# Norms by halves of the tokens, FFN width in three chunks and a ring of eight split weights, in a two-layer encoder trunk

## Chip, cores and metric

The kernel runs on one core of a Trainium2 chip. The metric is the device time of one execution in microseconds (us), the median of several runs of the kernel.

## The reference

Two layers over 576 tokens: 512 of a prompt and 64 of a sample with cached states, with the same weights. All is float32. Each sub-layer has a norm ahead of it and one behind it:

```python
h = rmsnorm(x, norm_pre[l, 0])
x = x + 0.5 * rmsnorm(swiglu(h, ffn1_gu[l], ffn1_down[l]), norm_post[l, 0])
h = rmsnorm(x, norm_pre[l, 1])
...
mix = jnp.concatenate([sb_out, conv_out, o_hg], axis=-1) @ w_out[l]
x = x + rmsnorm(mix, norm_post[l, 1])
h = rmsnorm(x, norm_pre[l, 2])
x = x + rmsnorm(memory_attention(h, mem_k[l], mem_v[l], w_mq[l], w_mo[l]), norm_post[l, 2])
h = rmsnorm(x, norm_pre[l, 3])
x = x + 0.5 * rmsnorm(swiglu(h, ffn2_gu[l], ffn2_down[l]), norm_post[l, 3])
```

`rmsnorm(x, g)` is x · rsqrt(mean(x²) + eps) · g over the 1024 features, and `swiglu` is (silu(h W_gate) · (h W_up)) W_down with a width of 2816. The mixer between `h @ w_in` (26 × 128 columns) and `w_out` has a stick-breaking attention, a short convolution and a gated recurrence. The memory attention has keys and values of 256 memory tokens (`w_mk`, `w_mv`, from a normed memory) for the prompt and cached ones for the sample.

## The kernel before

All activations are feature-major: a tile [128, 8, 576] holds 8 blocks k of 128 features for 576 tokens. A float32 product is made of three fp32r products: weights and activations are split into a high and a low part, and hi·hi, lo·hi and hi·lo are added up in PSUM.

A **unit** is 128 output features of one projection. Its weights (128 × 1024 for 8 blocks k, 128 × 1408 for half of the FFN's width) are loaded into `raw` by SyncE's queue; ScalarE rounds them to `w_hi` (L855), VectorE subtracts to `w_lo` (L1183), and TensorE makes 3 products for each k and each half of the tokens (288 columns), 48 in all for 8 blocks k (`unit`, L372 to L390). The ring has two places; ScalarE's and VectorE's `step(u)` split unit u + 1 when unit u is done (L862, L1189). For the memory's keys, values and queries there are three places.

The order of the work is written out by hand, engine by engine; each queue goes through the phases F1, D1 (FFN up and down), IN, mixer, OUT, MK, MV and MQ in turns, cross-attention, MO, F2, D2, twice. The FFNs are loops (`Fori`).

At the end of a sub-layer every output tile is squared by ScalarE from PSUM (L906), GpSimd adds the squares up (L1597) and VectorE scales the tile by its gain into y (L1222). Behind the last unit, TensorE sums over the features by one-column products (`mean_square`, L411), ScalarE estimates the root by Ln and Exp (L900, L901), VectorE refines it (L1209 to L1214), TensorE spreads it over the partitions (`spread`, L420), and ScalarE copies it to `rinv` (L903). Then, for each k and all 576 tokens, y·rinv is made by VectorE for even k (L1227) and by GpSimd for odd k (L1605), VectorE updates x (L1231), ScalarE makes h_hi (L888) and the square for the next norm (L889), VectorE makes h_lo (L1196). The first unit of the next block waits for h_hi and h_lo per k:

```python
def h_gate(pn):
    def gate(ready, k):
        pe.wait_ge(ready, KD * pn + k + 1)
    return gate
```

The norm ahead of a sub-layer multiplies outputs, not h: its root is made beside the second unit (L401) and applied when a tile leaves PSUM. Around MK the updates stand between the units' splits on VectorE. The transposes of the sample's cached keys and of the new memory rows stand between the score products of the cross-attention (L782, L791). At the end, x is transposed (L832) and stored per block of 128 tokens.

## Time and profile before

| | |
|---|---|
| median of 3 runs | 3103.36 us (3102.82 to 3107.18) |
| span of the profiled execution | 3090.4 us |
| median less that span | 13.0 us |
| TensorE busy (20794 products) | 2920.0 us, 94% |
| VectorE, ScalarE, GpSimd busy | 1311.8, 943.6, 293.7 us |
| DMA | 232.84 MB, mean 75 GB/s |

The span is the time from the first to the last instruction of one profiled execution; no other time of that execution was recorded, so the median stands for it in the third line. Busy time is the time that an engine has an instruction under way; engines overlap, so the shares don't add up. The chain of work that ended last is followed back from the last instruction, and a wait is put down to the instruction that released it. The granted clock is the share of TensorE's full speed that the throttle allowed.

### The profile page before, as it was taken

Reading aid. Unit: us, or ns where it says so; the run is one execution under the profiler, and the core shown is the slowest. Engines: PE = TensorE matmul, PEld = TensorE weight load, DVE = VectorE, ACT = ScalarE, POOL = GpSimd, SP = SyncE. Lnnn points to the kernel's source line nnn. Section 1 sums busy time; section 2 is a strip of 40 time slices with the busy share of each in tenths; the row PEclk is TensorE's granted clock in tenths of the full one; section 3 lists DMA queues with packets and bytes.
Section 4 is the critical chain, followed back from the end, with each engine's and each line's share of the span. In section 5 each row is a group of like instructions: output and inputs, shape, how many; then the busy total and the mean of one; then the engine's idle time right before and its main releaser. Section 6 shows DMA issues by size and latency. Waiting matters only on the chain.

```text
span 3090.4 us, 49001 instructions
## 1 busy us (share of the span) xinstructions
PE 2920.0 (94%) x20794; PEld 2761.1 (89%) x20794; DVE 1311.8 (42%) x1583; ACT 943.6 (31%) x1218; POOL 293.7 (10%) x185
## 2 busy tenths in 40 slices
PE   8999998999989979999899999799999988999997
PEld 7999998985788879999899999799758978999996
DVE  5444226733363364442354432456343634544322
ACT  3222213225443232222232221232253432322211
POOL 1000012000120120000210001300102103100011
PEclk9999998997999989999899999799889998999998
DMA  3222221220242113232222232122203411222321
GB/s 111 81 81 87 85 75 56 62 88 21 75 123 89 45 51 88 82 89 85 65 68 81 81 88 85 46 76 62 88 1 103 124 61 55 68 81 81 88 85 50
DMA packets 420836, 232.84 MB, mean 75 GB/s; under 512 B 7076, under 2 KB 415688, under 8 KB 420712
## 3 DMA queue, kind: packets, MB, share of 16 engines
q1 hardware_dynamic: 414544, 210.33, 23.5%
q0 software_dynamic: 5936, 20.59, 1.9%
q8 instruction: 100, 1.64, 0.2%
q14 instruction: 24, 0.20, 0.0%
q10 hardware_dynamic: 232, 0.08, 0.0%
HBM read 219.44 MB, written 11.54 MB: 75 GB/s over the span
## 4 chain that ended last, share of the span: by engine, by line
PE 88%; DVE 7%; ACT 3%; issue 1%; DMA 1%; ACTq 0%; POOL 0%; DVEq 0%; POOLq 0%
PE PS L387 73%; DVE x L1231 2%; DVE y L1227 2%; PE PS L635 2%; PE PS L366 2%; DVE h_lo L1196 1%; PE PS L810 1%; PE PS L759 1%; PE PS L657 1%; PE PS L519 1%; PE PS L682 1%; DVE w_lo L1183 1%; PE PS L420 1%; PE PS L660 1%; PE PS L411 1%
## 5 line engine op out<-in xcount | busy, mean ns | idle before, releaser
L1183 DVE TENSOR_TENSOR w_lo<-raw,w_hi 128x1024 fp32r<-128x1024 f32 (+1 forms) x372 | 482.3, 1297 | 1271.4 <-ACT w_hi L855 1271.1
L387 PE MATMUL PS<-h_lo,w_hi 128*128 128x288 f32 x3904 | 848.1, 299 | 49.9 <-DVE h_lo L1196 49.6
L387 PE MATMUL PS<-h_hi,w_hi 128*128 128x288 f32 x3904 | 851.3, 300 | 26.0 <-ACT h_hi L888 21.5
L387 PE MATMUL PS<-h_hi,w_lo 128*128 128x288 f32 x3904 | 844.4, 298 | 0.0
L855 ACT ACTIVATE w_hi<-raw 128x1024 fp32r<-128x1024 f32 (+1 forms) x372 | 414.2, 1113 | 1246.8 <-PE PS L387 1246.4
L387 PEld LDWEIGHTS PS<-h_lo,w_hi 128*128 128x128 f32 x3904 | 635.9, 191 | 59.3 <-DVE h_lo L1196 59.3
L387 PEld LDWEIGHTS PS<-h_hi,w_hi 128*128 128x128 f32 x3904 | 638.2, 192 | 30.0 <-issue 22.3
L387 PEld LDWEIGHTS PS<-h_hi,w_lo 128*128 128x128 f32 x3904 | 638.8, 192 | 0.0
L1597 POOL TENSOR_TENSOR acc<-acc,sq 128x576 f32<-128x576 f32 x104 | 205.4, 1975 | 1862.6 <-ACT sq L906 1775.6
L387 PE MATMUL PS<-a_lo,w_hi 128*128 128x288 f32 x1408 | 300.4, 295 | 0.0
L387 PE MATMUL PS<-a_hi,w_lo 128*128 128x288 f32 x1408 | 300.3, 295 | 0.0
L387 PE MATMUL PS<-a_hi,w_hi 128*128 128x288 f32 x1408 | 300.2, 295 | 0.0
L387 PEld LDWEIGHTS PS<-a_hi,w_hi 128*128 128x128 f32 x1408 | 226.2, 188 | 0.0
L387 PEld LDWEIGHTS PS<-a_hi,w_lo 128*128 128x128 f32 x1408 | 226.2, 188 | 0.0
L387 PEld LDWEIGHTS PS<-a_lo,w_hi 128*128 128x128 f32 x1408 | 226.2, 188 | 0.0
L927 ACT ACTIVATE a_hi<-ut 128x576 f32 (+1 forms) x88 | 60.4, 687 | 258.8 <-DVE ut L1253 258.8
L920 ACT ACTIVATE sg<-gt 128x576 f32<-128x576 f32 x88 | 60.4, 687 | 176.1 <-DVE gt L1247 176.1
L1256 DVE TENSOR_TENSOR a_lo<-ut,a_hi 128x576 f32 (+1 forms) x88 | 66.7, 758 | 83.1 <-ACT a_hi L927 83.1
L366 PE MATMUL PS<-m_hi,w_hi 128*128 128x256 f32 x256 | 74.8, 292 | 12.7 <-DVE w_lo L1183 8.9
L1231 DVE SCALAR_TENSOR_TENSOR x<-y,x 128x576 f32<-128x576 f32 x64 | 85.7, 1352 | 1.1
L888 ACT ACTIVATE h_hi<-x,par 128x576 fp32r<-128x576 f32 x64 | 49.6, 775 | 96.1 <-DVE x L1231 87.9
L1222 DVE TENSOR_SCALAR y<-PS,par 128x576 f32<-128x576 f32 x64 | 52.0, 812 | 52.1 <-ACT sq L906 52.1
(286 smaller groups left out, 2843.7 us busy)
## 6 DMA issues: line engine op xcount, KB each, us to landing
raw<-in_ffn_gu_dram SPq DMA_DIRECT2D x176, 512.0 KB, 3.8
raw<-in_ffn_down_dram SPq DMA_DIRECT2D x64, 704.0 KB, 4.7
raw<-in_w_in_dram SPq DMA_DIRECT2D x52, 512.0 KB, 3.8
raw<-in_w_out_dram SPq DMA_DIRECT2D x16, 512.0 KB, 3.8
raw<-in_w_mk_dram SPq DMA_DIRECT2D x16, 512.0 KB, 3.8
raw<-in_w_mv_dram SPq DMA_DIRECT2D x16, 512.0 KB, 4.1
raw<-in_w_mq_dram SPq DMA_DIRECT2D x16, 512.0 KB, 3.9
raw<-in_w_mo_dram SPq DMA_DIRECT2D x16, 512.0 KB, 3.8
```

Source lines behind the costliest of these rows:

```text
L366: m = mm(out, lhs(a, k), rhs(b, k), start=(first and n == 0), stop=(last and n == 3 * kt - 1))
L387: m = mm(PL[slot][:, h, 0:HT], wt(ws)(a, k), (hi, lo)[b][:, k0 + k, h * HT:(h + 1) * HT], start=(first and n == 0), stop=(last and n == 3 ...
L635: mm(z[:, Z_OFF[j]:Z_OFF[j] + SEQ - j * P], proj[e:e + 64, K0 + h // 2, j * P:(j + 1) * P], proj[e:e + 64, Q0 + h // 2, j * P:SEQ], start= ...
L855: A(whi(s, slice(0, words)), rawu(s, slice(0, words)), ACT.Copy).then_inc(whi_r, 1)
L920: A(sg[:, :], gt[:, :], ACT.Silu).then_inc(sg_r, 1)
L927: A(a_hi[:, bass.ds(r, 1), :], ut[:, :].rearrange("p (o t) -> p o t", o=1), ACT.Copy).then_inc(ahi_r, 1)
L1183: TT(wlo(s, c), rawu(s, c), f32(whi(s, c)), ALU.subtract).then_inc(wlo_r, 1)
L1222: TS(halves(y[:, m, :]), PL[m % 2][:, :, 0:HT], gpost(l, pn % 4, m), None, ALU.mult).then_inc(tile_e, 1)
L1227: TT(y[:, k, :], y[:, k, :], rinv[:, :], ALU.mult).then_inc(y_r, 1)
L1231: STT(x[:, k, :], y[:, k, :], weight, x[:, k, :], ALU.mult, ALU.add).then_inc(x_r, 1)
L1256: TT(a_lo[:, bass.ds(r, 1), :], ut[:, :].rearrange(o1, o=1), f32(a_hi[:, bass.ds(r, 1), :]), ALU.subtract).then_inc(alo_r, 1)
L1597: nc.gpsimd.tensor_tensor(acc[:, :], acc[:, :], sq[:, c % 2, :], ALU.add).then_inc(acc_r, 1)
```

## The change

- **Halves.** Norm statistics, `rinv`, x, h_hi and h_lo are kept by halves of the tokens (288 each) with semaphores per half. The last projection of a sub-layer (the FFN's last down chunk, MO) runs all 8 units for the first half and then all 8 for the second (`ends_by_halves`); the next block begins with 8 (FFN) or 6 (IN) units for the first half and then for the second (`begins_by_halves`). A step of one half has 24 products and one PSUM bank. While TensorE makes the second half of the down product, the first half's norm and update go on; while it makes the first half of the next block, those of the second half. `PIECES` says beside which step which k is updated.
- **Norm.** Gains are applied with `rinv` in one instruction (`scale_y`), squares are taken of y in SBUF and added by VectorE (`add_square`), and the root is a bit estimate with three Newton steps on VectorE (`inverse_root`). Mean square and spread are products per half set between the products of a step. Every root is made by token now, that of the norm ahead of a sub-layer too.
- **Weights.** A unit has at most 8 blocks k; a ring of eight places holds split weights, with three `raw` buffers; tables built when the program is written say which unit is split after which step (5 and 3 steps ahead where units go by halves, else 3 and 2; a place must be free). In MK, MV and MQ the ring has three places.
- **FFN.** The width goes in chunks of 6, 8 and 8 blocks: gate and up, then a down product of the chunk, whose partial sums VectorE adds into y (`take_y`). All loops are written out.
- **Mixer to memory.** OUT keeps full width. The memory's transposes go beside OUT, the updates (`piece`) beside the 16 MK and MV units, then come 8 MQ units, with the transposes of cached keys and memory rows beside them.
- **GpSimd** only starts transfers. The output leaves per block of tokens, the first half's ahead.

The core of the diff:

```diff
-PHASES = [("F1", 2 * KF, KD), ("D1", 2 * KD, KU), ("IN", NIN, KD), ("OUT", KD, KD), ("MK", KD, KD),
-          ("MVQ", 2 * KD, KD), ("MO", KD, KD), ("F2", 2 * KF, KD), ("D2", 2 * KD, KU)]
+CHUNKS = (6, 8, 8)
...
+LAG_F, LAG_IN = 8, 6
+RING = 8
...
+        at_h = max(at_h, HELD[u], FIRST[u] - (5 if by_halves else 3))
+        at_l = max(at_l, at_h, FIRST[u] - (3 if by_halves else 2))
...
+PIECES = [(), (0,), (1, 2), (3,), (4, 5), (6,), (7,), ()]
...
+            def begins_by_halves(l, name, pn, lag):
+
+                post = 2 * pn - 1
+                for j in range(lag):
+                    beside = {}
+                    if j == 0 and pn:
+                        beside = {6: lambda: mean_square(post, 1)}
+                    elif j == 1:
+                        beside = {1: lambda: mean_square(2 * pn, 0), 6: lambda: spread(2 * pn, 0)}
+                        if pn:
+                            beside[3] = lambda: spread(post, 1)
+                    step(l, name, j, 0, h_hi, h_lo, gate=h_gate(pn, (0,)) if j == 0 else None, beside=beside)
+                for j in range(lag):
+                    beside = {}
+                    if j == 0:
+                        beside = {4: lambda: mean_square(2 * pn, 1)}
+                    elif j == 1:
+                        beside = {2: lambda: spread(2 * pn, 1)}
+                    step(l, name, j, 1, h_hi, h_lo, gate=h_gate(pn, (1,)) if j == 0 else None, beside=beside)
...
+            def inverse_root(r, a, t):
+
+                link(TS(r.bitcast(I32), a.bitcast(I32), 1, None, ALU.logical_shift_right))
+                link(TS(r.bitcast(I32), r.bitcast(I32), -1.0, ROOT_BITS, ALU.mult, ALU.add))
+                for n in range(3):
+                    link(TT(t, r, r, ALU.mult))
+                    link(STT(t, t, -0.5, a, ALU.mult, ALU.mult))
+                    ins = STT(r, t, 1.5, r, ALU.add, ALU.mult)
...
+            def ends_by_halves(l, name, pn, y_, weight, take):
...
+                for m in range(KD):
+                    turn(done(l, name, m, 1))
+                    take(m, 1)
+                    if m:
+                        add_square(n, m - 1, 1)
+                    for k in PIECES[m]:
+                        piece(pn + 1, k, 0, y_, weight)
+                    if m == 6:
+                        finish(pn + 1, 0)
+                add_square(n, KD - 1, 1)
+                newton(n, 1)
...
+                for n in range(2 * KD):
+                    turn(done(l, "MK" if n < KD else "MV", n % KD))
+                    if n == 1:
+                        piece(pn + 1, 0, 0, yh, 1.0)
+                        piece(pn + 1, 0, 1, yh, 1.0)
+                    elif n:
+                        piece(pn + 1, n // 2, n % 2, yh, 1.0)
```

Three places show how instructions moved. First TensorE, at the end of layer 0's first FFN. Before, the norm's products stood behind the last down unit and ahead of the first product of IN:

```order
L387 MATMUL PS<-a_lo,w_hi 128x288 x2
L411 MATMUL PS<-cst,acc 128x1 x5
L411 MATMUL PS<-cst,sq 128x1 x5
L420 MATMUL PS<-cst,small 128x128 x4
L420 MATMUL PS<-cst,small 128x64
L387 MATMUL PS<-h_hi,w_hi 128x288 x2
L387 MATMUL PS<-h_hi,w_lo 128x288 x2
L387 MATMUL PS<-h_lo,w_hi 128x288 x2
```

Now, in the first pass of IN (steps 0 and 1, first half; L449 is the mean square, L457 the spread):

```order
L432 MATMUL PS<-h_lo,w_hi_104 128x288
L449 MATMUL PS<-cst,acc 128x1 x3
L432 MATMUL PS<-h_hi,w_hi_104 128x288
...
L432 MATMUL PS<-h_lo,w_hi_105 128x288
L449 MATMUL PS<-cst,acc 128x1 x3
L432 MATMUL PS<-h_hi,w_hi_105 128x288
...
L457 MATMUL PS<-cst,small 128x128 x2
L457 MATMUL PS<-cst,small 128x32
L432 MATMUL PS<-h_hi,w_hi_105 128x288
```

The second half's norm behind the FFN is finished between products of IN's first half. Then VectorE behind the same down product; before, with the root's refinement (L1209 to L1214), one split and the updates of whole rows of tokens:

```order
L1222 TENSOR_SCALAR y<-PS,par 128x576 [waits square_ready,unit_products_done]
L1209 TENSOR_SCALAR small<-PS 128x5 [waits mean_square_ready]
L1211 TENSOR_TENSOR small<-small 128x5 [waits root_estimated]
L1212 TENSOR_TENSOR small<-small 128x5 [waits vector_step]
L1213 TENSOR_SCALAR small<-small 128x5 [waits vector_step]
L1214 TENSOR_TENSOR small<-small 128x5 [waits vector_step]
L1183 TENSOR_TENSOR w_lo<-raw,w_hi 128x1024 [waits w_hi_ready]
L1227 TENSOR_TENSOR y<-y,rinv 128x576 [waits rinv_ready]
L1231 SCALAR_TENSOR_TENSOR x<-y,x 128x576 [waits even_y_scaled]
L1231 SCALAR_TENSOR_TENSOR x<-y,x 128x576 [waits odd_y_scaled]
L1196 SCALAR_TENSOR_TENSOR h_lo<-x,par,h_hi 128x576 [waits h_hi_ready]
```

Now, one step of the second half of the down product (L1244 splits a weight, L1386 takes the step's tile into y, L1257 adds a square, L1286 scales y, L1297 updates x, L1280 makes h_lo; 0 and 1 at a semaphore's name are the halves):

```order
L1244 TENSOR_TENSOR w_lo_112<-raw_118,w_hi_104 128x1024 [waits w_hi_ready,step_products_done]
L1386 TENSOR_TENSOR y<-y,PS 128x288 [waits psum_tile_emptied]
L1257 TENSOR_TENSOR acc<-acc,sq 128x288 [waits squares_added1,square_ready1]
L1286 SCALAR_TENSOR_TENSOR y<-y,par,rinv 128x288
L1297 SCALAR_TENSOR_TENSOR x<-y,x 128x288 [waits y_scaled0]
L1280 SCALAR_TENSOR_TENSOR h_lo<-x,par,h_hi 128x288 [waits h_hi_ready0]
L1257 TENSOR_TENSOR acc<-acc,sq 128x288 [waits squares_added0,square_ready0]
```

The update of the first half stands between the takes of the second half. Last, VectorE in the memory's units; before:

```order
L1183 TENSOR_TENSOR w_lo<-raw,w_hi 128x1024 [waits w_hi_ready,unit_products_done]
L1227 TENSOR_TENSOR y<-y,rinv 128x576
L1231 SCALAR_TENSOR_TENSOR x<-y,x 128x576 [waits even_y_scaled]
L1196 SCALAR_TENSOR_TENSOR h_lo<-x,par,h_hi 128x576 [waits h_hi_ready]
L1183 TENSOR_TENSOR w_lo<-raw_93,w_hi 128x1024 [waits w_hi_ready,unit_products_done]
L1231 SCALAR_TENSOR_TENSOR x<-y,x 128x576 [waits odd_y_scaled]
```

and now:

```order
L1244 TENSOR_TENSOR w_lo_114<-raw_117,w_hi_106 128x1024 [waits w_hi_ready,step_products_done]
L1286 SCALAR_TENSOR_TENSOR yh<-yh,par,rinv 128x288
L1297 SCALAR_TENSOR_TENSOR x<-yh,x 128x288 [waits y_scaled0]
L1280 SCALAR_TENSOR_TENSOR h_lo<-x,par,h_hi 128x288 [waits h_hi_ready0]
L1257 TENSOR_TENSOR acc<-acc,sq 128x288 [waits squares_added0,square_ready0]
L1244 TENSOR_TENSOR w_lo_115<-raw_118,w_hi_107 128x1024 [waits w_hi_ready,step_products_done]
```

Each unit has the piece of one half now, over 16 units in place of 8, and the squares are added here and not on GpSimd.

## Rows read from the trace of the kernel before

**Rows 1.** The page: busy time of the engines, and the chain's shares by engine

```profile
PE 2920.0 (94%) x20794; PEld 2761.1 (89%) x20794; DVE 1311.8 (42%) x1583; ACT 943.6 (31%) x1218; POOL 293.7 (10%) x185
...
PE 88%; DVE 7%; ACT 3%; issue 1%; DMA 1%; ACTq 0%; POOL 0%; DVEq 0%; POOLq 0%
```

**Rows 2.** Waits of TensorE: us in total, times, longest

```profile
PE PS L387 <- DVE h_lo L1196: 49.6, 21, 2.7
PE PS L387 <- ACT h_hi L888: 21.5, 5, 4.3
```

**Rows 3.** Timeline of TensorE from F1 to IN: start, duration, instruction, wait

```profile
452.14 1.17 PE L411 MATMUL PS<-cst,acc 128*128 128x1 f32 x10
...
456.11 2.69 PE L420 MATMUL PS<-cst,small 128*128 128x128 f32 x10 [1.60 <-DVE small L1214]
463.10 0.82 PE L387 MATMUL PS<-h_hi,w_hi 128*128 128x288 f32 x2 [4.30 <-ACT h_hi L888]
...
476.32 0.85 PE L387 MATMUL PS<-h_lo,w_hi 128*128 128x288 f32 x2 [2.63 <-DVE h_lo L1196]
```

**Rows 4.** Windows: length, busy by engine, granted clock, DMA share, GB/s

```profile
463.10:488.70 25.60, 16.04 (x57) 14.06 (x58) 23.28 (x19) 10.95 (x16) 17.67 (x11) 0.51 0.01 3
488.70:495.10 6.40, 6.40 (x49) 6.34 (x48) 3.58 (x6) 1.80 (x3) 0.00 (x0) 1.00 0.28 82
...
1083.20:1118.50 35.30, 19.84 (x90) 17.31 (x88) 28.87 (x28) 14.52 (x22) 20.45 (x11) 0.56 0.05 15
```

**Rows 5.** Timeline of VectorE at the same boundary

```profile
455.28 0.17 DVE L1211 TENSOR_TENSOR small<-small 128x5 f32<-128x5 f32 x1 [0.57 <-ACT small L901]
455.48 0.17 DVE L1212 TENSOR_TENSOR small<-small 128x5 f32<-128x5 f32 x1
...
467.82 1.83 DVE L1231 SCALAR_TENSOR_TENSOR x<-y,x 128x576 f32<-128x576 f32 x1
469.58 0.81 DVE L1196 SCALAR_TENSOR_TENSOR h_lo<-x,par,h_hi 128x576 fp32r<-128x576 f32 x1
470.31 0.75 DVE L1231 SCALAR_TENSOR_TENSOR x<-y,x 128x576 f32<-128x576 f32 x1
...
487.56 1.22 DVE L1183 TENSOR_TENSOR w_lo<-raw,w_hi 128x1024 fp32r<-128x1024 f32 x1 [2.10 <-ACT w_hi L855]
```

**Rows 6.** Groups by line: busy us, mean ns of one, idle before and releaser

```profile
L1253 DVE TENSOR_TENSOR ut<-ut,sg 128x576 f32<-128x576 f32 x88 | 66.7, 758 | 10.1
L888 ACT ACTIVATE h_hi<-x,par 128x576 fp32r<-128x576 f32 x64 | 49.6, 775 | 96.1 <-DVE x L1231 87.9 <-DVE x L1280 7.4
L889 ACT ACTIVATE sq<-x 128x576 f32<-128x576 f32 x56 | 37.4, 669 | 0.0
L1482 DVE TENSOR_TENSOR at_c<-at_s,at_c 128x256 f32<-128x256 f32 x16 | 6.8, 424 | 0.6
```

**Rows 7.** Timeline of ScalarE at the same boundary

```profile
486.40 1.06 ACT L855 ACTIVATE w_hi<-raw 128x1024 fp32r<-128x1024 f32 x1 [2.18 <-PE PS L387]
```

**Rows 8.** Windows from OUT's end to MQ's end, columns as above

```profile
855.00:897.00 42.00, 33.30 (x240) 31.30 (x238) 34.19 (x40) 25.77 (x44) 16.20 (x12) 0.88 0.39 113
897.30:974.00 76.70, 75.75 (x580) 75.07 (x580) 30.93 (x31) 21.06 (x28) 1.15 (x1) 1.00 0.41 117
```

**Rows 9.** Timeline of TensorE in layer 0's cross-attention

```profile
974.80 7.17 PE L759 MATMUL PS<-mk_p,qx 128*128 128x256 f32 x32 [0.85 <-DVE qx L1544]
...
991.76 3.72 PE L759 MATMUL PS<-mk_p,qx 128*128 128x256 f32 x16 [0.69 <-ACT mv_p L1134]
```

**Rows 10.** Timeline of the end of the program

```profile
3056.26 1.17 PE L411 MATMUL PS<-cst,acc 128*128 128x1 f32 x10
...
3075.29 1.43 DVE L1231 SCALAR_TENSOR_TENSOR x<-y,x 128x576 f32<-128x576 f32 x2
```

**Rows 11.** The chain in order of time: two FFN's up products, start, length, count

```profile
37.11 415.20 PE PS L387 x3114
...
1118.87 404.93 PE PS L387 x3114
```

More of the change, by code:

```diff
@@ L583, in _ @@
                         beside[6] = head_squares
[L584 to L587 removed]
+                    step(l, "IN", m, None, h_hi, h_lo, beside=beside)
+                pe.wait_ge(tile_e, emptied(l, "IN", NIN - 2))
                 pe.wait_ge(hu_r, l + 1)
```

1170 lines of the change are left out of this document (597 added, 573 removed).

## The prediction

> **What bounds the kernel now.** The page's busy line and its chain of waits come first [rows 1]: TensorE is busy for 94% of the span, and 88% of the chain that ended last is TensorE. So only two things can move the time: time in which TensorE waits, and time in which it works below full clock. The table of waits [rows 2] says where it waits: 49.6 us for h_lo in 21 waits and 21.5 us for h_hi, both at the first unit after a sub-layer. The timeline of one such boundary [rows 3] shows the order: the down product ends at 452.14, the norm's small matmuls follow, the first product of the next block starts at 463.10, and then TensorE stops before pair after pair (2.63 us at 476.32). The table by windows [rows 4] has the second half of the loss: in 463.10 to 488.70 the granted clock is 0.51, the 1.2 GHz level, and right behind it, where products come without waits, it is 1.00, the 2.4 GHz level. From 452.1 to 488.7 are 36.6 us, in which 54 products of 0.133 us, 7.2 us, got done [rows 3, 4, 11]: a loss of 29.4 at such a boundary into the mixer (2 of them). Into an FFN it is 35.3 − 7.2 = 28.1 us (3 of them) [rows 4]. These five, 143 us, and the end of the program are what the change can gain. The same windows show VectorE busy for 23.28 of 25.60 us [rows 4], so VectorE sets that stretch.
>
> The unit of my sum is the profiled execution's span, 3090.4 us; the median of the three runs is 3103.36, 13.0 above it, and I carry these 13.0 over. Below 0.2%, 6 us, a measurement of this kernel can't be told from no change.
>
> **Prices of VectorE's halves.** 576 columns take 0.758 us and 256 take 0.424 [rows 6], so 1.04 ns a column and 0.16 us fixed: 288 columns take 0.46. With a gain from a pointer 0.81 for 576 becomes 0.51, and the x update 0.75 becomes 0.45 [rows 5]. Operations behind each other start 0.08 us before the end of the one ahead (469.58 + 0.81 against 470.31) [rows 5]. One piece, that is scale, x, h_lo and sum of squares for a half, is then 0.51 + 0.45 + 0.51 + 0.46 − 4 × 0.08 = 1.61 us. Before, the same x update took 1.83 us beside GpSimd's product and 0.75 without it [rows 5]; GpSimd computes nothing in the new kernel, so the low price holds throughout. The root is a chain of 12 tiny operations, each waiting for the one ahead, at the 0.20 us from 455.28 to 455.48 [rows 5]: 2.4 us, with the hand-overs around it 2.6, four times per boundary.
>
> The Trainium skill speaks against the halves (VectorE: DVE Perf Modes, section The TRN2 errata — SBUF-src ops pay a fixed extra latency per instruction): the latency is paid between instructions, so many small tiles pay it each, and it advises 512 elements or more. The 0.16 us fixed agree with that; the 0.08 by which a successor overlaps does not, and the sum goes by the rows. By the rule in full a piece is 1.93 and the sum 3049 in place of 3029: rival 2.
>
> **One boundary after the change.** Let 0 be the end of the down product's first half. The second half's 8 steps take 25.6 us (24 × 0.133 = 3.2 each), with norm matmuls in them about 27.1. The first half's root is ready at 4.9, spread and copied at 6.3, and the pieces begin behind the second take of y, at 8.0. From there VectorE has 6 takes (0.37), 6 sums (0.38), 8 pieces (12.5, since the first square needs no sum) and 4 splits (1.22 − 0.08 each) [rows 5]: 21.6 us, so it ends at 29.6. ScalarE makes h_hi and the squares in halves (0.78 and 0.67 us for the whole [rows 6]) between its splits of 1.06 [rows 7]; four such splits may each hold a piece up, by 0 to 1 us, I take 0.5: 31.6. TensorE wants the second half's mean square at k = 6 of the next block's first step, at 29.1 with its own detours: **a stall of 2.5 us**. Behind it, root (2.6), a split and another root stand in VectorE's line; TensorE reaches the first spread 2.0 and the second 1.2 us later, so 1.2 and 2.4 more. The second half's pieces, 12.5 plus 6 takes and a split, 16 us, run beside the rest of the first pass (14.8 us): about 1.0 at the mean square and 0.6 at the last spread. Stalls: 7.7. TensorE's four mean squares and spreads are 12 products of one column and 12 of 128: at 0.12 and, at the low level, 0.27 each [rows 3] 4.7 us, and about 3 at the high one; I take 3.4. For clock dips near the stalls I add 2.0. **Loss 13 us**, against 29.4 and 28.1. Gain 2 × 16.4 + 3 × 15.1 = 78. Bounds: stalls gone but the 3.4 and 1 left, 4.4; stalls and the low level, next part.
>
> **Memory keys and values.** Now the mixer's output norm runs in the 16 MK and MV units, one piece each. The order below the diff shows that unit n + 3's w_lo stands ahead of unit n's piece, and both its splits wait for unit n. Per unit: w_hi 1.06, w_lo 1.15, scale 0.43, x 0.37, ScalarE's h_hi and square 0.77, and some hand-overs: 3.9 us, where TensorE's 24 products of 256 columns, by their columns, need 2.84. So 16 × 3.9 + 10 for the two roots ahead = 73, and MQ (8 × 6.4, one wait of some 5 us) ends at 129.5, plus 2 for the memory's transposes beside OUT, against the 119.0 from 855 to 974 before [rows 8]. The cached keys' transposes move beside MQ: before, they stood between two score products, 9.8 us from 981.97 to 991.76 [rows 9]. Two MO splits queue ahead of the last query tile: 3.3. Net 12.5 − 9.8 + 3.3 = +6 a layer, **+12** (bounds −6 to +14 each: no lock-step at all, or TensorE at the low level for two units).
>
> **Start and end.** At the start a split and a root stand ahead of step 1's spread (1.2 + 2.6 + 0.7 copy): **+4.5**, 0 to 6. At the end, x's last tile was ready at 3076.7, 20.5 us behind the last product at 3056.26 [rows 10]; now 5.5 for the norm and 8 × 0.80 for scale and x make 11.9. What follows was 13.7 for five blocks of tokens; with three left 9.6. **−12.6** (−6 to −16).
>
> **Edits at nothing.** 32 more splits and the partial sums of y (16 per FFN at 0.76) lie beside steps of 4.8 and 6.4 us; if their cover went, 0.76 each, 49 us. Between chunks TensorE reaches the last k of a down step at 4.0 to 5.6 us, a_lo is there at about 4.3. Products and their weight loads are as many as before (a load stands with every matmul already). Loops unrolled: products inside the loops already come each 0.133 us [rows 11], so nothing. The other pace, 0.130 [rows 11], appears in one FFN of four; all four so would be −31, none +10.
>
> **Sum**: −78 + 12 + 4.5 − 12.6 = −74; 3103.4 − 74 = **3029 us**, own range 2998 to 3055.
>
> **Rivals.**
> 1. *Cover complete.* VectorE keeps up, MK and MV don't lock. For: 29.6 stands close to 29.1. Against: roots in one line with splits. Loss 4.4 per boundary: −(2 × 25.0 + 3 × 23.7) = −121, memory part −6.4 × 2 = −13, rest −8: 2961.
> 2. *Every half pays in full.* No overlap: 0.32 a piece, 2.6 us a pass, 8 passes with stalls: +20, 3049. For: the 0.16 fixed. Against: the 0.08. This is the page's rule.
> 3. *Some steps at the low level.* A step at 1.2 GHz costs 3.2 us more. With three such per boundary in place of the dips: 5 × 9.6 − 10 = +38: 3067.
> 4. *Slower: the low level from the first wait to the last.* Before, the clock stayed at 0.51 from the first wait to the last [rows 4]. After, waits stand from the next block's step 0 to the second pass's step 0: 6 steps into the mixer, 8 into an FFN, 2 × 6 + 3 × 8 = 36 steps, 115 us. Without dips the change gains 74 + 10 = 84, so it loses from 27 steps on; this gives 3103 − 84 + 115 = 3134. Against: between these waits lie 4 to 6 steps without any, and in 488.70 to 495.10 the level was 1.00 at once.
> 5. *The halves don't overlap at all*, since a wait holds a whole pass: the root's chain is merely moved, and the memory part cancels the end: 3100.
>
> **Chances.** Forecast 0.45, rival 1 0.23, 2 0.10, 3 0.09, 4 0.10, 5 0.03. Faster: 0.45 + 0.23 + 0.10 + 0.08 = 0.86; same 0.03; slower 0.11 (rival 4, 0.01 of 3). The range 2960 to 3085 takes in rivals 1 to 3 and leaves out 4, 5 and a tail below.
>
> **What would show it.** The waits for h_lo and h_hi at products nearly vanish; in their place stand waits of mean square and spread for acc and small, under 10 us per boundary. GpSimd has no arithmetic. In the windows of the new boundaries the clock is above 0.85. w_lo in MK and MV comes each 3.9 us. The last output leaves 22 us after the last product. I am wrong if a boundary loses over 20 us, if TensorE waits at down steps for y's takes or for splits, or if the clock stays near 0.5 in a by-halves pass.

## The result, and the profile after

The kernel takes **3051.09 us** (median of four runs, 3047.48 to 3056.27) against 3103.09 of the kernel before on the same chip: a ratio of **0.985, interval 0.9825 to 0.9875**. It is faster by 52 us, where 74 were forecast, and 3051 lies inside the forecast's own range.

The page, the line of the engines and the chain's shares [rows 1]:

```profile
PE 2922.1 (96%) x20906; PEld 2768.8 (91%) x20906; DVE 1442.7 (47%) x2585; ACT 971.1 (32%) x1456; POOL 32.0 (1%) x50
...
PE 87%; DVE 5%; ACT 3%; issue 3%; DMA 1%; ACTq 0%; DVEq 0%; POOL 0%; POOLq 0%
```

TensorE is busy for as long as before in a span of 3051.4 us, 39 shorter than that of before. GpSimd has only its transfers left. TensorE's waits (us in total, times, longest) [rows 2]:

```profile
PE PS L449 <- DVE acc L1257: 29.8, 14, 3.8
PE PS L412 <- ACT mk_p L1164: 11.7, 12, 1.5
PE PS L412 <- ACT mvT L1164: 10.5, 12, 0.9
...
PE PS L432 <- ACT a_hi L1003: 2.9, 4, 0.7
```

The 71 us of waits for h_hi and h_lo are gone, as the prediction's last part asked for; the mean square (L449) waits for its sum of squares instead. The windows of TensorE's waits, the products behind them and the stretch after that, from F1 to IN (length, busy by engine, granted clock, DMA share, GB/s) [rows 4]:

```profile
466.20:470.00 3.80, 0.16 (x2) 0.00 (x0) 3.21 (x6) 2.00 (x4) 0.71 (x1) 1.00 0.37 105
470.00:479.60 9.60, 9.58 (x49) 9.13 (x49) 7.09 (x30) 0.41 (x1) 0.00 (x0) 0.64 0.37 111
479.60:494.80 15.20, 15.20 (x117) 15.20 (x116) 13.87 (x33) 7.15 (x17) 0.00 (x0) 1.00 0.13 37
```

TensorE stands for 3.8 us, then works 9.6 us at a mean granted clock of 0.64, so that 0.36 / 0.5 of them, 6.9 us, were at 1.2 GHz; and then 2.4 GHz holds, where before 25.6 us were at 0.51. At the boundary from layer 0's second FFN to layer 1's first, the stretch behind a wait of 3.8 us:

```profile
1532.80:1543.80 11.00, 10.96 (x48) 10.55 (x48) 7.13 (x30) 2.26 (x3) 0.00 (x0) 0.53 0.31 91
```

By the same working 10.3 us are at 1.2 GHz here. Counted alike in both kernels (from 192 products ahead of the down's end to the 288th product of IN, or the 384th of an FFN, less 0.1333 us a product), a boundary into IN lost 29.6 us and now 13.7, one into an FFN 27.5 to 28.4 and now 14.9 to 15.9.

**Two paces.** One thing had to be taken out before stages could be compared. The chain's longest rows, the run of an FFN's gate and up products with the down products of its first two chunks (the rows of before [rows 11] hold down products too), read in the kernel after and in one of the experiments (newton2):

```profile
67.97 341.80 PE PS L432 x2562
```

```profile
1548.52 333.81 PE PS L432 x2562
...
2602.97 341.80 PE PS L432 x2562
```

The same 2562 products take 0.1334 or 0.1303 us each, at a granted clock of 1.00 both, and one program shows both in one execution. A whole FFN at the faster pace is 8 to 10 us shorter. The profiled execution of before had one such FFN of four (404.93 against 415.20 [rows 11]), that of after none; newton2 and late_pieces below have three. So stages are compared at the slower pace: 0.16 us are added for every 48 FFN products made at the faster one. The sums are then 3100.4 before and 3053.2 after, **47.2** apart; the rest of the 52 is put down to pace. (After has no fast FFN, yet its sum is 1.8 above its span: some of the half steps, at 0.1316 us a product in every kernel by halves, are counted as fast.) In this measure (stage ends at its last product; us):

| stage | before | after | mk_pieces_first | three_edits | three_edits + idle products |
|---|---|---|---|---|---|
| F1 and D1, layer 0, with the start | 452.1 | 464.3 | 463.6 | 465.1 | 463.5 |
| IN, layers 0 / 1 | 235.4 / 235.4 | 217.3 / 217.4 | 217.9 / 218.7 | 217.2 / 214.1 | 215.4 / 214.2 |
| mixer and OUT | 167.4 / 167.5 | 165.4 / 161.8 | 161.8 / 163.3 | 165.8 / 163.6 | 163.5 / 162.2 |
| MK, MV, MQ | 118.8 / 118.8 | 135.3 / 135.3 | 114.3 / 113.1 | 113.1 / 115.9 | 114.3 / 114.3 |
| cross-attention, MO | 109.3 / 109.2 | 106.2 / 106.2 | 106.3 / 107.7 | 107.7 / 109.8 | 106.5 / 106.6 |
| F2 and D2, layer 0 | 450.5 | 439.0 | 439.1 | 438.0 | 434.7 |
| F1 and D1, layer 1 | 450.8 | 440.0 | 439.9 | 438.1 | 434.6 |
| F2 and D2, layer 1 | 450.8 | 439.0 | 439.4 | 437.9 | 434.7 |
| behind the last product | 34.2 | 26.3 | 26.0 | 25.7 | 26.2 |
| sum | 3100.4 | 3053.2 | 3011.0 | 3011.8 | 2990.6 |

The last column is three_edits_filler. The mixer's stage scatters between executions of kernels that don't differ there, and with its clock: 153.9 us in late_pieces (layer 1), where 10.2 us of it are at 1.2 GHz, 161.8 in the kernel after (27.3) and 168.8 in masks_after_x (44.4). Two sums less than 15 us apart are therefore read at their boundaries, whose losses add up to 142.9 us before and 73.3 after. The memory's part, 33 us slower in the two layers, is the one place where the change costs a lot.

### The profile page after: what moved, and what is told of

Its sections match the earlier page's. It is cut to its first block, busy times and chain, and to the rows that moved or that the text cites. A ratio compares the mean times of both kernels' runs of the same rounds, so it can differ in the third digit from the quotient of the medians.

```text
span 3051.4 us, 48442 instructions
## 1 busy us (share of the span) xinstructions
PE 2922.1 (96%) x20906; PEld 2768.8 (91%) x20906; DVE 1442.7 (47%) x2585; ACT 971.1 (32%) x1456; POOL 32.0 (1%) x50
## 3 DMA queue, kind: packets, MB, share of 16 engines
q1 hardware_dynamic: 415056, 210.33, 23.9%
## 4 chain that ended last, share of the span: by engine, by line
PE 87%; DVE 5%; ACT 3%; issue 3%; DMA 1%; ACTq 0%; DVEq 0%; POOL 0%; POOLq 0%
PE PS L432 72%; ACT w_hi L912 2%; PE PS L681 1%; PE PS L836 1%; PE PS L868 1%; DVE w_lo L1244 1%; PE PS L703 1%; PE PS L457 1%; PE PS L566 1%; PE PS L728 1%; PE PS L449 1%; DVE x L1297 1%; PE PS L706 1%; DVE acc L1257 1%; DVE yh L1286 1%
## 5 line engine op out<-in xcount | busy, mean ns | idle before, releaser
L1244 DVE TENSOR_TENSOR w_lo<-raw,w_hi 128x1024 fp32r<-128x1024 f32 (+1 forms) x404 | 485.4, 1203 | 1162.3 <-PE PS L432 845.3
L432 PE MATMUL PS<-h_hi,w_hi 128*128 128x288 f32 x3904 | 911.4, 300 | 4.6 <-DVE x L1428 3.0
L432 PE MATMUL PS<-h_lo,w_hi 128*128 128x288 f32 x3904 | 899.8, 297 | 0.0
L432 PE MATMUL PS<-h_hi,w_lo 128*128 128x288 f32 x3904 | 899.8, 297 | 0.0
L1003 ACT ACTIVATE a_hi<-ut 128x576 fp32r<-128x576 f32 (+1 forms) x104 | 63.5, 610 | 151.8 <-DVE ut L1376 151.8
L1000 ACT ACTIVATE sg<-gt 128x576 f32<-128x576 f32 (+1 forms) x104 | 63.5, 611 | 137.5 <-DVE gt L1370 137.4
L1257 DVE TENSOR_TENSOR acc<-acc,sq 128x288 f32<-128x288 f32 x224 | 99.6, 450 | 2.3 <-ACT sq L941 2.0
L935 ACT ACTIVATE h_hi<-x,par 128x288 fp32r<-128x288 f32 x128 | 68.3, 534 | 100.2 <-DVE x L1297 88.2
L412 PE MATMUL PS<-m_hi,w_hi 128*128 128x256 f32 x256 | 75.7, 296 | 22.2 <-ACT mk_p L1164 11.7
L1363 DVE TENSOR_TENSOR a_lo<-ut,a_hi 128x576 fp32r<-128x576 f32 (+1 forms) x104 | 68.7, 661 | 39.7 <-PE PS L432 30.7
L1386 DVE TENSOR_TENSOR y<-y,PS 128x288 f32<-128x288 f32 (+1 forms) x96 | 52.8, 550 | 57.5 <-PE PS L432 57.5
L432 PE MATMUL PS<-xo_hi,w_hi 128*128 128x288 f32 x256 | 76.0, 297 | 3.6 <-DVE xo_lo L1705 3.6
```

What stands on the lines that cost most here:

```text
L412: m = mm(out, wt[a][:, k * P:(k + 1) * P], (hi, lo)[b][:, k0 + k, :], start=(n == 0), stop=(n == 3 * KT[u] - 1))
L432: m = mm(BK[bank][:, 0:HT], wt[a][:, k * P:(k + 1) * P], (hi, lo)[b][:, k, c * HT:(c + 1) * HT], start=(n == 0), stop=(n == 3 * kt - 1))
L935: A(h_hi[:, k, cols(h)], x[:, k, cols(h)], ACT.Copy, scale=gpre(pn // 4, pn % 4, k)).then_inc(hi_r[h], 1)
L1000: A(sg[:, cols(h)], gt[:, cols(h)], ACT.Silu).then_inc(sg_r, 1)
L1003: A(a_hi[:, u // 2, cols(h)], ut[:, cols(h)], ACT.Copy).then_inc(ahi_r, 1)
L1244: TT(w_lo[SLOT[u]][:, c], raw[u % 3][:, c], f32(w_hi[SLOT[u]][:, c]), ALU.subtract).then_inc(wlo_r, 1)
```

## The experiments

All are edits of the changed kernel; ratios stand to the kernel before.

### mk_pieces_first: the memory's circle broken on VectorE

```diff
                 for n in range(2 * KD):
-                    turn(done(l, "MK" if n < KD else "MV", n % KD))
                     if n == 1:
                         piece(pn + 1, 0, 0, yh, 1.0)
...
+                    turn(done(l, "MK" if n < KD else "MV", n % KD))
```

> In the memory's 16 units VectorE updates x (scale, x, h_lo, sum) ahead of the unit's split and no longer behind it. Theory, lock-step: the 3.98 us from one w_lo to the next (865.82, 869.80, 873.78) are one circle, w_hi on ScalarE, w_lo, scale and x on VectorE, h_hi and square on ScalarE; with the update ahead, w_hi and the update go side by side, VectorE needs 1.60 + 1.15 = 2.75 and TensorE's 2.84 decides: 14 units x 1.1 = 15 us a layer, 31 us in all, about 3021. Rival, evacuation: TensorE's waits are for ScalarE's copies of mk_p and mvT (11.7 and 10.5 us); the copies stay behind w_hi, so the waits stay and nothing changes (within 5 us). Rival, the wait moves: MQ's start waits for the roots anyway and gives half back, 15 us.

Measured: 3012.26 us (3009.19 to 3021.05), **0.9743 [0.9707, 0.9778]**; 3011.0 at the slower pace, 42 less than the changed kernel, where 31 were expected. MK, MV and MQ take 21 and 22 us a layer less. VectorE in the units of MK, in the changed kernel (start, duration, instruction, wait):

```profile
869.80 1.23 DVE L1244 TENSOR_TENSOR w_lo<-raw,w_hi 128x1024 fp32r<-128x1024 f32 x1 [1.53 <-ACT w_hi L912]
870.94 0.51 DVE L1286 SCALAR_TENSOR_TENSOR yh<-yh,par,rinv 128x288 f32<-128x288 f32 x1
871.37 0.45 DVE L1297 SCALAR_TENSOR_TENSOR x<-yh,x 128x288 f32<-128x288 f32 x1
...
873.78 1.23 DVE L1244 TENSOR_TENSOR w_lo<-raw,w_hi 128x1024 fp32r<-128x1024 f32 x1 [1.52 <-ACT w_hi L912]
```

ScalarE in the same units:

```profile
871.86 0.54 ACT L935 ACTIVATE h_hi<-x,par 128x288 fp32r<-128x288 f32 x1 [1.89 <-DVE x L1297]
872.30 0.43 ACT L936 ACTIVATE sq<-x 128x288 f32<-128x288 f32 x1
872.63 1.04 ACT L912 ACTIVATE w_hi<-raw 128x1024 fp32r<-128x1024 f32 x1
873.58 0.36 ACT L1164 ACTIVATE mk_p<-PS 128x256 f32<-128x256 f32 x1
```

The split waits for w_hi, w_hi stands behind the square of x, x stands behind the last split: 3.98 us around, with both engines waiting for each other 1.5 to 1.9 us each time. The copy that empties TensorE's bank goes around with it, and that is the wait for mk_p and mvT. VectorE of this experiment has no such wait, and its splits come 2.87 us apart:

```profile
867.93 1.23 DVE L1244 TENSOR_TENSOR w_lo<-raw,w_hi 128x1024 fp32r<-128x1024 f32 x1
...
870.81 1.23 DVE L1244 TENSOR_TENSOR w_lo<-raw,w_hi 128x1024 fp32r<-128x1024 f32 x1
```

The window of 13 units, in which TensorE has no gap (columns as above):

```profile
857.90:895.30 37.40, 37.40 (x314) 37.40 (x313) 35.96 (x64) 27.38 (x53) 0.00 (x0) 1.00 0.64 183
```

So 2.87 is what TensorE needs. Of the 21 us, 15 are the units (67.2 to 52.5 us from MK's start to MQ's) and 6 are MQ behind them (67.9 to 61.7). Those 6 are a stall and the clock again. In MQ of the changed kernel:

```profile
920.34 0.83 PE L449 MATMUL PS<-cst,acc 128*128 128x1 f32 x6 [3.13 <-DVE acc L1257]
```

```profile
920.30:929.00 8.70, 8.66 (x44) 8.66 (x45) 4.70 (x27) 1.06 (x1) 0.00 (x0) 0.61 0.15 43
```

The last updates come late there, TensorE waits 3.13 us for their sum of squares, and 6.8 us behind the wait are at 1.2 GHz, which costs 3.4. In this experiment there is no wait at that place, and the clock stays at 1.00.

### mk_copy_first: the same stage, the other engine

```diff
-                    turn(done(l, "MK" if n < KD else "MV", n % KD))
+                    act.wait_ge(unit_d, done(l, "MK" if n < KD else "MV", n % KD))
                     A((mk_p if n < KD else mvT)[:, n % KD, :], PL[n % 2][:, 0, 0:NMEM], ACT.Copy).then_inc(mkv_e, 1)
+                    turn(done(l, "MK" if n < KD else "MV", n % KD))
```

> In the same units ScalarE copies mk_p and mvT out of PSUM ahead of the next w_hi and not behind it. Rival, evacuation: TensorE's 22.2 us of waits for these copies go, 3029. Theory, lock-step: the circle of 3.98 us doesn't hold the copy's place (0.36 us lie beside VectorE's work), w_hi even comes 0.36 us later in it; the waits only change their name, to w_lo: 0 to +10 us.

Measured: 3053.64 us (3040.72 to 3059.47), 0.9866 [0.9827, 0.9905]; MK, MV and MQ 139.7, 4.4 longer a layer. Expected was that the waits for the copies would go or turn into waits for w_lo; they stay, 26.8 us against 22.2. The copy stands behind the square of x now and so still goes around with the circle, which grows by it from 3.98 to 4.24 us (w_lo at 868.90 and 873.14). That the wait for mk_p is a sign of the circle and no cause of its own is shown by mk_pieces_first: there the copies stand behind w_hi as in the changed kernel, and TensorE waits for none.

### late_pieces: the overlap taken away

```diff
-PIECES = [(), (0,), (1, 2), (3,), (4, 5), (6,), (7,), ()]
+PIECES = [(), (), (), (), (), (), (), (0, 1, 2, 3, 4, 5, 6, 7)]
...
-                    if m == 6:
+                    if m == 7:
                         finish(pn + 1, 0)
```

> All eight updates of the first half stand behind the last take of the second pass (one change of the table, with the last h_lo behind them): the cover of the second pass is taken away, the rest of the change stays. Theory, cover is what the change gains: 12.5 us of VectorE's work per boundary come onto TensorE's path, at half clock in part: 5 x 12 to 15 us, 60 to 75 us more, about 3118. Rival, the gain is from GpSimd's arithmetic gone and shorter instructions: the first products of the next block need the updates only k by k, 1.6 us each against 0.4 us of products: 5 x 5, 25 us more, about 3078.

Measured, a single run: 3079.45 us with three FFNs at the faster pace, 3102.6 at the slower one. That is 49 above the changed kernel and 2 above the one before; expected were 60 to 75 more, or 25. A boundary loses 24.2 to 24.8, 10 more (49 in all), the end takes 7 longer, and the mixer of layer 1 happened to be 8 shorter. TensorE at the first boundary:

```profile
466.24 0.58 PE L432 MATMUL PS<-h_hi,w_hi 128*128 128x288 f32 x1 [3.94 <-ACT h_hi L935]
...
469.63 0.61 PE L432 MATMUL PS<-h_lo,w_hi 128*128 128x288 f32 x1 [0.51 <-DVE h_lo L1280]
...
477.12 1.44 PE L449 MATMUL PS<-cst,acc 128*128 128x1 f32 x6 [2.09 <-DVE acc L1257]
```

The waits for h_hi and for pair after pair of h_lo are back [rows 3], those for h_lo shorter (0.5 us for 2.7 at most). So 49 of the 70 us that the boundaries gained are the updates beside the down product's second half. The other 20 stay without that overlap: a boundary still loses less than the 27.5 to 29.6 of before, with 20.5 to 23.9 us at 1.2 GHz where before there were 30.7 to 34.1. Which part of the change brings these 20 (halves, the new root, no arithmetic on GpSimd), no run separates. The whole time is back at that of before because the memory's part and the start cost about as much as these 20 give.

### squares_first, hi4, newton2: what makes the stall

The chain that ended last through the stall (start, length, what):

```profile
464.21 3.80 DMA raw<-in_w_in_dram
...
469.05 0.43 ACT sq L941
469.51 0.47 DVE acc L1257
470.02 0.83 PE PS L449 x6
470.85 1.85 PE PS L432 x9
472.70 1.07 PE PS L449 x6
473.77 1.65 PE PS L432 x6
475.42 1.42 PE PS L457 x6
476.84 2.01 PE PS L432 x9
478.84 0.78 PE PS L457 x6
479.62 15.24 PE PS L432 x114
```

A weight's load ends ahead of ScalarE's last square, and this gave two theories: the load holds ScalarE's queue up, or VectorE has too much ahead of the last sum. squares_first puts the squares ahead of the splits:

```diff
-                    turn(s + 1)
                     post_square(pn, y_, s, m, 1)
+                    turn(s + 1)
...
-                    turn(done(l, name, m, 1))
+                    v.wait_ge(unit_d, done(l, name, m, 1))
                     take(m, 1)
                     if m:
                         add_square(n, m - 1, 1)
+                    if m == KD - 1:
+                        add_square(n, KD - 1, 1)
+                    turn(done(l, name, m, 1))
```

> In the second pass of a down product VectorE takes y and adds squares ahead of its split, and ScalarE squares y ahead of its split; nothing else moves. Theory, a late weight: the 3.8 us stall at the mean square of the second half comes from a raw buffer freed late, whose load lands at 468.01 and holds ScalarE's queue, with the last square behind it; with the square ahead, the stall falls to about 1 us: 5 boundaries x 2.5 to 3, 12 to 15 us less, about 3037. Rival, VectorE's work (the step of the prediction): VectorE has 21.6 us of work from 8.0 on and more by hand-overs, so the end of the sums only changes its place with a split: 0 to 5 us less.

Measured: 3048.81 us (3045.83 to 3056.44), 0.986 [0.9824, 0.9896]; 3051.1 at the slower pace; waits for acc 27.3 us, the longest 4.3. The order alone does next to nothing: at four boundaries the stall is 2.8 to 2.9 us in place of 3.5 to 3.8, and the five lose 71.3 us in all against 73.3. At the first boundary, with the 4.3, a late load stood in ScalarE's queue one step earlier, so this left the load open.

hi4 lets ScalarE split four steps ahead where units go by halves, so that each load has a step more:

```diff
-        at_h = max(at_h, HELD[u], FIRST[u] - (5 if by_halves else 3))
+        at_h = max(at_h, HELD[u], FIRST[u] - (4 if by_halves else 3))
```

> Where units go by halves, w_hi is made 4 steps ahead and not 5; w_lo stays 3 ahead. So the raw buffer is asked for one step later, and its load (freed by the w_lo of three units before, 3.8 us to landing) is there when ScalarE comes to it. Theory, a late weight: ScalarE's waits for loads in the second passes (464.66 and 468.09 at the first boundary) go, the last square comes in time, and the stall at the second half's mean square (3.8 us) falls to about 1: 12 us less in all at the same pace of the products. Rival, VectorE's work: 21.6 us from 8.0 on are there whatever ScalarE does; the stall keeps 2.5 us or more: 0 to 6 us less.

Measured: 3035.70 us (3026.68 to 3048.87), 0.9799 [0.976, 0.9838]; 3048.4 at the slower pace, with 72.0 us at the boundaries. ScalarE's 66.5 us of waits for the weights of down, MO and IN are gone, and the stall is not: 26.8 us in 14 waits. VectorE ahead of one, and TensorE's wait:

```profile
1084.83 1.21 DVE L1244 TENSOR_TENSOR w_lo<-raw,w_hi 128x1024 fp32r<-128x1024 f32 x1
...
1088.66 1.22 DVE L1244 TENSOR_TENSOR w_lo<-raw,w_hi 128x1024 fp32r<-128x1024 f32 x1
1089.80 0.45 DVE L1708 COPY yh<-PS 128x288 f32<-128x288 f32 x1
1090.16 1.05 DVE L1257 TENSOR_TENSOR acc<-acc,sq 128x288 f32<-128x288 f32 x2
```

```profile
1091.27 1.44 PE L449 MATMUL PS<-cst,acc 128*128 128x1 f32 x6 [3.04 <-DVE acc L1257]
```

VectorE has no gap up to the last sum, and TensorE waits 3.04 us for it, here and at the other four boundaries: the bound that the prediction named, without any load. The load that ended in the chain only came on top.

newton2 leaves out one of the root's three Newton steps (its output is coarser), 3 of 12 chained operations:

```diff
-                for n in range(3):
+                for n in range(2):
...
-                    if n < 2:
+                    if n < 1:
                         link(ins)
```

> Two Newton steps per root and not three (so a coarser root): each chain of tiny operations loses 3 x 0.20 = 0.6 us. Theory of the prediction (the roots stand in line on TensorE's path, two of them behind the stall of each boundary): 2 x 0.6 per boundary, 2 x 0.6 at each layer's memory part, 0.6 at start and end: 6 + 2.4 + 1.2 = about 10 us less at the same pace. Rival, the roots are covered by products: 0 to 2 us less.

Measured: 3031.92 us (3021.40 to 3037.63), 0.9788 [0.9756, 0.9821], with three FFNs of the profile at the faster pace; 3049.7 at the slower one, 3.5 less than the changed kernel. Boundaries into an FFN lose 13.8 to 15.1 against 14.9 to 15.9, those into IN 13.4 and 14.2 against 13.7: 1.8 less in all five, where 6 were expected if the roots stood on the path. The 3.5 of the sum is less than the mixer's scatter, so no more than those 1.8 can be read.

### squares_gpsimd: the arithmetic given back to GpSimd

```diff
-                add_square(2 * pn, k, h)
...
+                        nc.gpsimd.tensor_tensor(acc[:, cols(h)], acc[:, cols(h)], sq[:, k % 2, cols(h)], ALU.add).then_inc(acc_r[h], 1)
```

> The squares of the norm ahead of a sub-layer are added by GpSimd again (112 of 224 sums), VectorE makes the others. VectorE is rid of 14 x 0.37 = 5.2 us per boundary. Theory of the prediction (low prices hold since GpSimd computes nothing): beside a GpSimd sum, VectorE's half operations grow as 0.75 grew to 1.83, that is 0.45 to about 1.1; a sum takes GpSimd about 1.0, so some 14 us of VectorE's time per boundary run at less than half speed, 8 us more than is saved... in all 10 to 25 us slower than the changed kernel at the same pace. Rival, rid of a quarter of its work VectorE is earlier: up to 15 us faster.

Measured, a single run: 3040.49 us, 3055.6 at the slower pace, 2.4 above the changed kernel, and 73.3 us at the boundaries, as there. GpSimd's half sums (busy us, mean ns), and a sum and a split of VectorE beside one:

```profile
L1726 POOL TENSOR_TENSOR acc<-acc,sq 128x288 f32<-128x288 f32 x112 | 111.0, 991 | 1672.2 <-ACT sq L936 1671.9
```

```profile
443.08 0.70 DVE L1257 TENSOR_TENSOR acc<-acc,sq 128x288 f32<-128x288 f32 x1
...
454.33 1.81 DVE L1244 TENSOR_TENSOR w_lo<-raw,w_hi 128x1024 fp32r<-128x1024 f32 x1
```

VectorE's sum alone is 0.45, its split 1.22. What it is spared, 0.37 a sum, it would pay in stretched neighbours; that they make up for all of it isn't shown. "No arithmetic on GpSimd" shows no gain by itself in this one run.

### masks_after_x: the start

The bounds and masks, which the changed kernel casts ahead of the copies of x, go behind all but the last split of the start:

```diff
-            nc.vector.tensor_copy(lmask[:, :, :], lst[:, 0:LEVELS, :])
...
-            for u in LOW_AT[0][2:]:
-                split(u)
+            for u in LOW_AT[0][2:-1]:
+                split(u)
...
+            nc.vector.tensor_copy(lmask[:, :, :], lst[:, 0:LEVELS, :])
...
+            split(LOW_AT[0][-1])
```

> VectorE's small work on the gate's bounds and the masks (11.67 to 14.06) stands behind the first half's h_lo and no longer ahead of the copies of x, as in the kernel before. Theory: the first product comes 2.4 us earlier after the gains' transposes, and the first steps keep that: 2 to 3 us less. Rival: the raw load that lands at 33.09 decides the start; then 0 to 1 us. Seen in the trace from the transposes of the gains on, since the load ahead of them varies by some us from run to run.

Measured, a single run: 3056.2 us. The time from the gains' arrival to the first product is 14.4 in place of 16.6 us, 2.2 less; the arrival itself differed by 2.6 between the two executions, so the total can't show it.

### filler, three_edits, three_edits_filler: the clock

filler lets TensorE make 20 products on old operands, into a bank that is free, ahead of the mean square for which it waits:

```diff
+                def kept_busy():
+                    for _ in range(20):
+                        mm(BK[2][:, 0:HT], w_hi[SLOT[UNIT[l, name, 0]]][:, 0:P], h_hi[:, 0, 0:HT], start=True, stop=True)
+                    mean_square(post, 1)
...
-                        beside = {6: lambda: mean_square(post, 1)}
+                        beside = {6: kept_busy}
```

> Ahead of the mean square of the second half, at which TensorE waits 3.0 to 3.8 us, it makes 20 products that nobody reads (2.7 us, extra work into a spare bank); all else is the changed kernel. Theory, the low level has a price of its own: behind the stall 9 products take 1.85 to 2.4 us where 1.2 would do, the one-column products and spreads double too; with TensorE busy through the stall the clock stays at 1.00, the stretch from the mean square to the second spread (9.6 us at the first boundary) shrinks to about 6.5, and a boundary gains 3: 15 us less in all at the same pace. Rival, the roots decide: the chain mean square, root, split, root on VectorE has the same length at either clock, TensorE waits at the spreads instead: 0 to 4 us less. Rival, the products come too late or too many: 0 to 10 us more.

Measured: 3037.91 us (3027.83 to 3051.26), 0.9833 [0.9793, 0.9873]; 3047.3 at the slower pace. Boundaries lose 11.9, 16.5, 12.4, 12.3 and 14.4. At three the clock stayed at 1.00, and they are better by 1.4 to 3.5. At two it fell all the same, for 10.2 and 6.8 us; one is worse by 1.6, the other better by 0.5. Waits of 1.1 to 1.9 us were left behind the idle products everywhere, 1.9 and 1.3 at the two, 1.1, 1.2 and 1.5 at the three. Alone it doesn't decide. So the stall was first made shorter: three_edits is mk_pieces_first, hi4 and squares_first together.

> Three edits together: the memory's updates ahead of the splits, w_hi 4 steps ahead where units go by halves, and in a down product's second pass the takes and squares ahead of the splits on VectorE and ScalarE. Theory, VectorE's work sets the stall, and without a late load in ScalarE's queue the order counts: behind the last take stands no split of 1.15 us any more, so the stall falls from 3.0 to about 1.9, 5 x 1.1 = 5 us below the first edit alone: 3006 us at the slow pace. Rival, the order doesn't count, the sum of the work does: as the first edit alone, 3011 at the slow pace.

Measured: 2991.83 us (six runs, 2982.60 to 2998.50), 0.9666 [0.9638, 0.9694]; 3011.8 at the slower pace, no less than mk_pieces_first alone. The waits for acc are halved (14.8 us in 12; 1.9 at each boundary for 3.5 to 3.8 in mk_pieces_first), and yet four boundaries of five lose 13.6 to 14.0, only 0.3 to 1.8 less than there: behind the shorter stall, too, 10.2 us are at 1.2 GHz. The fifth, into IN of layer 1, has the same stall of 1.91 us, but only 3.4 us at 1.2 GHz, and loses 10.4. So the clock's share shows within one execution.

three_edits_filler has 14 idle products in that kernel:

> As three_edits, with 14 products that nobody reads (1.9 us) ahead of the second half's mean square. Theory of the clock's price: 3 us less per boundary than three_edits, 15 in all, about 2990 at the slow pace. Rival, the roots decide: as three_edits, within 4 us.

Measured: **2984.06 us** (six runs, 2973.10 to 2990.04), **0.9645 [0.9618, 0.9672]**, the shortest of all, 67 under the changed kernel; 2990.6 at the slower pace, 21.2 less than three_edits. All five boundaries lose 10.2 to 10.7, 3.4 less at the four where three_edits lost 13.6 to 14.0. That is 14 of the 21; the rest stands in stages that have no idle products, the mixer's and MO's above all, and isn't claimed for them. The window behind the down's end from F2 to F1, without and with the idle products (columns as above):

```profile
1498.10:1514.00 15.90, 13.99 (x70) 13.31 (x69) 12.54 (x40) 6.29 (x10) 0.00 (x0) 0.68 0.41 116
```

```profile
1497.00:1509.20 12.20, 11.19 (x82) 10.36 (x81) 11.30 (x38) 6.00 (x9) 0.00 (x0) 1.00 0.50 145
```

From the down's end to the long run of products (at 1513.73 and 1509.22) are 15.6 us at 0.68 and 12.2 at 1.00. And what the low clock had hidden comes up, in the waits of the second kernel for the root:

```profile
PE PS L457 <- DVE small L1271: 6.9, 7, 1.9
```

At full clock TensorE reaches the second spread 0.95 us ahead of the root (L1271) at each of the five, which it never did at a boundary of the changed kernel (the longest wait of the row, 1.9, is at the start). For acc no wait of more than 0.3 us is left at a boundary.

## Why the prediction was right, and where it was wrong

At the slower pace of both kernels:

| term | forecast | measured |
|---|---|---|
| five boundaries | −78 | −70 |
| chunks of the FFNs | 0 | +5 |
| memory part, two layers | +12 | +15.5 |
| start | +4.5 | +9.2 |
| end | −12.6 | −6.1 |
| not accounted for | | −0.8 |
| sum | −74 | −47 |

The boundaries are 2 × −15.9 and −12.6, −12.0 and −13.5. Each down's second pass has 1.83 us of norm products (27.43 for 25.60), counted at its boundary or, for the last one, at the end (−7.9 + 1.8). The last 1056 products of an FFN take 143.8 us for 140.8; without the 1.83 that leaves 1.2 for the chunks, four times. The memory part is +33.0 for MK to MQ, −7.7 for mixer and OUT, and −6.1 − 3.7 for MO without its norm products; the −7.7 are no more than the mixer's scatter.

Sign, mechanism and places were right: the loss lay at the boundaries, the overlap took 49 us of it away, as late_pieces shows, and another 20 went without it. The sizes were off in every term, and each the same way.

**The 13.0 around the span** was not what it was taken for. The executions after show 2.3 between time and span (3053.7 against 3051.4); some 10 of the rest were the one FFN at the faster pace in the profiled execution of before. Carrying the 13.0 over was right by luck, since after had no fast FFN.

**The piece** was priced at 1.61 and takes 1.59 (one begins at 456.31, the next at 457.90). Rival 2 had 1.93 and falls: there is a fixed share in each half, but a successor starts 0.06 to 0.08 us before the end of the one ahead. It was the prediction's reading, in full for every instruction, of the Trainium skill's rule on latency (VectorE: DVE Perf Modes, section The TRN2 errata — SBUF-src ops pay a fixed extra latency per instruction).

**The boundary, 13 against 14.6.** The stall came where and why it was put, 3.8 us for 2.5 (3.04 in hi4, without the late load). The two waits for roots behind it, 1.2 and 2.4, didn't come: TensorE worked there at the low clock and was late itself; at full clock one of 0.95 is there (three_edits_filler). The 1.6 for the second half's pieces came as 0.2 at most. The clock, put at 2.0, costs (1.00 − 0.64) × 9.6 = 3.5 us at the first boundary and (1.00 − 0.53) × 11.0 = 5.2 at the one shown into an FFN; three_edits_filler gets 3.4 back at each boundary at which 10.2 us had been at 1.2 GHz, less than the 5.1 of their halves, since the wait for the root comes up.

The norm's products, put at 3.4, take 6.8 to 7.0: so long are the pauses that four mean squares and four spreads make between the long products in three_edits_filler, at a clock of 1.00 and without waits and idle products. The prediction took a row's count for products, but the rows have two for each (x10 in [rows 3] for the 5 that the order of the kernel before lists, x6 here for 3), so its 0.12 and 0.27 us are half a product's price. Rival 1's floor of 4.4 is too low by as much.

With 3.7 for the stall, 6.8 for the norm and 3.5 for the clock the first boundary's 13.7 are accounted for. So the forecast had nearly the right sum out of wrong terms, in part by luck: some 5 too much for waits that didn't come, 1.2, 3.4 and 1.5 too little for the stall, the norm and the clock. It failed in reading rows as products, and in pricing a wait and the clock behind it apart from each other, though the clock falls behind a wait and decides whether the next wait is seen.

**Chunks of the FFN**, costed at nothing, take 1.2 us an FFN: four waits for a_hi (2.9 us in all) and four for a_lo (1.0) stand in the table of waits, the rest is the products' restart. The step that failed is "a_lo is there at about 4.3": it was set against the last k of the down step, and the first wait is for a_hi.

**The memory's part.** Lock-step and 3.9 us a unit were right (3.98). The prediction's sum for the units gave 73 and the trace 67.2; what it missed is MQ, put at 56.5 and 67.9 long. The forecast had 51.2 for products and one wait of some 5. Measured are the products, 6.2 for the transposes beside them and 3.5 for norm products, neither counted, the stall of 3.1 us for acc, 3.2 for the low clock behind it, and 1.0 of other waits. The windows of the two parts [rows 8]:

```profile
861.60:913.70 52.10, 40.31 (x314) 38.02 (x312) 35.54 (x65) 27.97 (x54) 0.00 (x0) 1.00 0.46 131
913.70:981.80 68.10, 63.88 (x456) 62.23 (x456) 23.40 (x50) 16.07 (x26) 0.00 (x0) 0.95 0.25 71
```

In the first TensorE is idle for 11.8 us at a granted clock of 1.00; the second's 0.95 is the stretch behind the stall. With one line moved (mk_pieces_first) this part is 4.5 and 5.7 us shorter than before instead of 16.5 longer. The order could be read from the diff when the forecast was made; the lock was priced and not questioned.

**The start.** The split and root ahead of the spread were counted. Not counted was what was moved ahead of x: 2.4 us of bounds and masks on VectorE (11.67 to 14.06), of which masks_after_x gets 2.2 back. Nor was the clock: TensorE waits 2.5 us at that spread, and from 37.8 to 44.6 the granted clock is 0.50, 3.4 us lost, where before it was 1.00 there. The spread's root waited behind a split that was 2.02 us late:

```profile
34.25 1.23 DVE L1244 TENSOR_TENSOR w_lo<-raw,w_hi 128x1024 fp32r<-128x1024 f32 x1 [2.02 <-ACT w_hi L912]
...
37.56 0.16 DVE L1266 SCALAR_TENSOR_TENSOR small<-small 128x3 f32<-128x3 f32 x1
```

**The end.** Updates took 6.5 (6.4 forecast). The norm took 7.2 for 5.5: TensorE waits 1.6 us for the last sum, and makes the first half's transposes (L879) between mean square and spread, so that the spread starts 0.6 us behind the root (3030.02). What follows took 12.6 for 9.6: it was scaled by the blocks of tokens that are left, but 7.1 of it stand behind the last issue of a transfer (3044.34), as 9.3 did before, and don't shrink with their number. TensorE and VectorE [rows 10]:

```profile
3027.51 3.28 PE L879 MATMUL PS<-cst,x 128*128 128x128 f32 x16
3030.58 1.30 PE L457 MATMUL PS<-cst,small 128*128 128x128 f32 x6
3032.37 0.95 DVE L1286 SCALAR_TENSOR_TENSOR y<-y,par,rinv 128x288 f32<-128x288 f32 x2 [2.34 <-ACT rinv L946]
...
3038.89 4.53 PE L879 MATMUL PS<-cst,x 128*128 128x128 f32 x20 [1.64 <-DVE x L1297]
```

**The rivals.** Rival 1 (cover complete) falls with the 29.8 us of waits for acc; even the best kernel loses 10.2 at a boundary and not 4.4. Rival 3 had the mechanism but two to three times the price: 6.9 to 10.3 us at 1.2 GHz a boundary cost 3.5 to 5.2, not 9.6. Rival 4 falls: the clock was at 1.00 again from 479.60 on, 9.6 us behind the wait's end. Rival 5 (no overlap at all) is late_pieces only in part: its 3102.6 is near the rival's 3100, but with boundaries that still lose 20 us less than before, and a memory part and a start that cost 25 where the rival let the memory's part cancel the end.

What stays open: what picks an FFN's pace. All six runs of three_edits lie 16 to 31 us below its sum at the slower pace with 2.3 around it, and none of the four of mk_pieces_first lies more than 4.1 below its own, so part of it hangs on the program. Which of the edits brings it, and how, no run here tells.

## What to carry to other kernels

Where two in-order engines feed each other around a loop, write the circle down (split, update, rounding, split) and add it up: if it is longer than the engine that should be the bound, look for an instruction to move out of it; here that was worth 42 us, more than any other edit. A short wait on TensorE is to be priced with the clock behind it, and if it can't be removed, idle products in it can keep the clock: at five boundaries of five where they covered it (three_edits_filler), at three of five where 1.1 to 1.9 us were left (filler). When a price is taken from a row, check against the program how many instructions its count stands for. Before stages of two kernels are compared, look at a stretch that is the same in both: if its pace differs, that part of the difference isn't the change's.
